# GpSimd computes the low parts of one group's input weights in a two-layer decoder step

## What is computed

```
for i in range(2):                       # layer 0: gated linear attention, layer 1: Mamba-2 SSD
    h = rmsnorm(x, pre_norm[i])
    proj = h @ w_in[i]                   # 1024 -> 3088 (layer 0), 1024 -> 5152 (layer 1)
    # layer 1: split proj into z, xBC, dt; causal conv of width 4 and SiLU on xBC;
    #          chunked scan over tokens with a state per head; y * silu(z); group norm
    y = mixer(proj) @ w_out[i]
    x = x + rmsnorm(y, post_norm[i])
```

## Time and profile before

| | us |
|---|---|
| median of 3 runs | 1502.0 |
| the three runs | 1498.67 to 1502.01 |
| profiled execution, whole | 1505.68 |
| span of its trace | 1503.9 |

### The profile page before, as it was taken

One profiled execution on the slowest core, in us unless ns is written; L12 is line 12 of the kernel. 1 busy time (PEld: TensorE's weight loads), 2 busy tenths in 40 slices (PEclk: granted clock), 3 DMA queues, 4 the chain that ended last, 5 costly groups with the idle time before them and its releaser, 6 DMA issues. The chain is left out here.

```text
span 1503.9 us, 31302 instructions
## 1 busy us (share of the span) xinstructions
PE 1417.1 (94%) x11554; PEld 1180.0 (78%) x11554; DVE 1166.2 (78%) x2591; ACT 839.9 (56%) x1877; POOL 239.0 (16%) x424
## 2 busy tenths in 40 slices
PE   5999999799999979999999999979999999999987
PEld 5889887667888759988888888767777777777765
DVE  4556587758877986898887898995879777588786
ACT  4745555366556545556665764663746556464453
POOL 5010122001422100121110221120112211000002
PEclk8999999999999979999999999999999999999999
DMA  6474567356576434448844764853585674555463
GB/s 191 126 227 136 169 175 219 98 165 189 140 194 204 123 98 131 144 108 229 240 131 134 238 181 124 243 143 86 168 247 156 161 216 119 167 158 174 132 190 64
DMA packets 283874, 245.77 MB, mean 163 GB/s; under 512 B 32664, under 2 KB 250876, under 8 KB 283052
## 3 DMA queue, kind: packets, MB, share of 16 engines
q1 hardware_dynamic: 273628, 209.36, 47.2%
q0 software_dynamic: 10096, 34.41, 8.7%
HBM read 183.02 MB, written 65.00 MB: 165 GB/s over the span
## 5 line engine op out<-in xcount | busy, mean ns | idle before, releaser
L1482 PE MATMUL bank<-h,w 128*128 128x268 f32 (+1 forms) x4752 | 836.0, 330 | 19.2 <-ACT w L867 13.0
L1482 PEld LDWEIGHTS bank<-h,w 128*128 128x128 f32 x4752 | 701.2, 191 | 96.9 <-issue 22.8
L883 DVE TENSOR_TENSOR w<-w_raw,w 128x1024 fp32r<-128x1024 f32 x132 | 160.9, 1219 | 42.9 <-ACT w L867 42.6
L852 PE MATMUL bank<-s_w_out,s_yt_hi 128*128 128x512 f32 (+2 forms) x544 | 168.1, 398 | 2.0 <-DVE s_ys L2600 1.7
L867 ACT ACTIVATE w<-w_raw 128x1024 fp32r<-128x1024 f32 x132 | 138.7, 1051 | 7.8 <-DMA w_raw<-in_ssd_w_in_dram 7.7
L1560 DVE SCALAR_TENSOR_TENSOR conv<-before_conv,cw,conv 128x260 f32<-128x260 f32 (+2 forms) x216 | 125.3, 580 | 4.3
L852 PEld LDWEIGHTS bank<-s_w_out,s_yt_hi 128*128 128x128 f32 (+2 forms) x544 | 95.9, 180 | 28.6 <-issue 2.5
L852 PE MATMUL bank<-g_w_out,g_ot_hi 128*128 128x512 f32 (+2 forms) x288 | 98.0, 429 | 1.7 <-DVE g_ot_lo L2118 1.7
L852 PE MATMUL bank<-s_w_out,s_yt_lo 128*128 128x512 f32 x240 | 94.7, 395 | 0.0
L2363 ACT ACTIVATE s_decay<-s_decay,t_ac 128x128 f32<-128x128 f32 (+1 forms) x288 | 85.5, 379 | 1.2
L1528 ACT ACTIVATE conv<-bank,cw 128x268 f32<-128x268 f32 (+1 forms) x72 | 45.8, 637 | 67.1 <-PE bank L1482 48.7
(11 more groups left out here) (259 smaller groups left out, 2460.7 us busy)
## 6 DMA issues: line engine op xcount, KB each, us to landing
w_raw<-in_ssd_w_in_dram SPq DMA_DIRECT2D x80, 512.0 KB, 4.3
w_raw<-in_gla_w_in_dram SPq DMA_DIRECT2D x48, 512.0 KB, 4.4
s_decay<-kept_acd SPq DMA_DIRECT2D x32, 512.0 KB, 6.3
w_raw<-in_ssd_w_out_dram SPq DMA_DIRECT2D x30, 512.0 KB, 4.2
g_chunk<-kept_gq SPq DMA_DIRECT2D x32, 448.0 KB, 5.4
s_chunk<-kept_sq SPq DMA_DIRECT2D x32, 384.0 KB, 4.8
kept_sq<-stage SPq DMA_DIRECT2D x80, 134.0 KB, 4.5
kept_sq<-stage SPq DMA_DIRECT2D x40, 256.0 KB, 4.9
```

Of the source, the lines that this page charges most:

```text
L852: last = pe.matmul(bank[0:r, :], yt[a][:, k, 0:r], wo[:, b, 512 * half:512 * half + 512], start=(k + a + b == 0), stop=(k == tiles - 1 and ...
L883: dve.tensor_tensor(self.part(i, 1), self.raw(i), hi, ALU.subtract).then_inc(self.w_lo, 1)
L1482: last = pe.matmul(bank[:, 0:n], w[:, p.tile % 2, a, k, :], h[:, b, k, c:c + n], start=(i == 0), stop=(i == len(terms) - 1))
```

## The change

The low parts of layer 1 group 0's 41 input tiles are made by GpSimd, with the same subtraction on the same operands. All other low parts, among them the output weights of that group, stay on VectorE. GpSimd's subtractions count up a semaphore of their own, `pool_lo`. Whoever waits for a low part (TensorE ahead of its 17th matmul, TensorE in the output products, SyncE before a reload) now waits through `wait_low`, which picks the semaphore by the tile and counts the low parts of that kind up to it. The task keeps its place in the list.

```
@@ gpsimd program
             if name == "piece" and at == [10, 0]:
                 gla.prepare(pool)
                 gla.first_samples(pool)
+            elif name == "low" and W.by_pool(*at):
+                W.pool_low(pool, *at)
@@ vector program
-            if name == "low":
+            if name == "low" and not W.by_pool(*at):
                 W.low(dve, *at)
@@ Weights
+    def by_pool(self, i):
+        kind, w = self.plan.weights[i]
+        return kind == "in" and self.plan.tiles[w][0:2] == (1, 0)
+
+    def wait_low(self, engine, i):
+        same = sum(self.by_pool(q) == self.by_pool(i) for q in range(i + 1))
+        engine.wait_ge(self.pool_lo if self.by_pool(i) else self.w_lo, same)
@@ Weights.load
         elif i >= RAW:
-            sp.wait_ge(self.w_lo, i - RAW + 1)
+            self.wait_low(sp, i - RAW)
@@ Weights.out_products
-                pe.wait_ge(self.w_lo, self.index[("out", (L, G, u, k))] + 1)
+                self.wait_low(pe, self.index[("out", (L, G, u, k))])
@@ Weights
+    def pool_low(self, pool, i):
+        pool.wait_ge(self.w_hi, i + 1)
+        pool.tensor_tensor(self.part(i, 1), self.raw(i), self.part(i, 0).bitcast(F32), ALU.subtract).then_inc(
+            self.pool_lo, 1)
@@ Pieces.project
-                pe.wait_ge(self.W.w_lo, self.W.index[("in", p.tile)] + 1)
+                self.W.wait_low(pe, self.W.index[("in", p.tile)])
```

More of the change, by code:

```diff
@@ L779, in __init__ @@
         self.raw_in = [sem(f"raw_in{i}") for i in range(RAW)]
-        self.w_hi, self.w_lo = sem("w_hi"), sem("w_lo")
+        self.w_hi, self.w_lo, self.pool_lo = sem("w_hi"), sem("w_lo"), sem("w_pool_lo")
         self.index = {w: i for i, w in enumerate(plan.weights)}
```

## The result

| | before | after |
|---|---|---|
| median of the runs | 1502.01 us (1498.67 to 1503.57, 4 runs) | 1532.25 us (1530.57 to 1533.24, 4 runs) |
| ratio, 95% interval | 1 | 1.0197 (1.0181 to 1.0214) |
| span of the profiled execution | 1503.9 us | 1531.2 us |
| mean granted clock of TensorE | 0.981 | 0.974 |

The kernel became 30 us slower. The forecast was 1505 us with a range up to 1514 us, so it was wrong by 27 us.

A forecast was written before the change was run, and what follows sets the result against it. TensorE, busy 94% of the span, was taken as the bound. Three places at +1.4, +1.8 and +1.2 us less 0.7 us gave +3.7 us on the 1502.0 us median: 1505.7, rounded down to 1505 us, range 1495 to 1514.

The forecast's parts named there:

- GpSimd's time: Length of each of the 41 subtractions of 128x1024 on GpSimd: 2.3 us, worked out from two smaller GpSimd instructions.
- second rival: GpSimd's instruction is longer, up to 3.7 us, so the kernel takes 1510 to 1514 us; slower cases together 0.34.
- other 38: The moved subtractions outside the three places on TensorE's path: taken as covered by three banks, at no cost.
- 1.08 us of the earlier trace: At 857.27 us a 0.19 us GpSimd operation took 1.08 us beside VectorE's subtraction; taken to show waiting in both directions.
- 54 us read off: VectorE's total wait, from placing 2.3 us subtractions at the 41 high parts in the timeline: 0 to 2.3 us each.
- three places: At 674, 723 to 726 and 771 us TensorE waits for VectorE behind a moved subtraction: +1.4, +1.8 and +1.2 us.
- shrinking gaps: Sign to check: gaps at 674, 726 and 771 us grow by 1 to 2 us; if they shrink, VectorE doesn't wait.
- balance of equal amounts: On VectorE, about 54 us of waits replace the 50.0 us of subtractions removed, so on the whole it gets nothing.
- 0.7 us had been counted as gained: TensorE's waits on the low-part subtraction L883, 0.7 us in all, would vanish; waits on GpSimd under 1 us.
- third rival: GpSimd's order makes low parts late behind samples or roots: +8 us at 41 x 0.2 us; little chance, within slower's 0.34.
- two DMA issues: Behind a sample's state update GpSimd's subtraction stands behind two issues of 0.76 us each; the added wait costed at nothing.
- TensorE's work plus its gaps: Sets the program's length: TensorE busy 94% of the span; the change removes none of its instructions, so only gaps count.

The follow-up runs named there:

- second: The changed kernel, but GpSimd makes the 41 low parts of layer 1's second group and VectorE those of the first; 1508.6 us.
- fourth: The changed kernel, but GpSimd makes the low parts of only every fourth input weight of the first group, 10 of the 41; ratio 1.0035.
- relief: The kernel before, but VectorE computes only 8 of 1024 values of each of the 41 low parts, the rest not computed; 1491.6 us.
- block: The kernel before, all low parts on VectorE, with GpSimd subtracting a 128x512 tile from itself twice beside each of the 41, for nobody; 1539.1 us.
- late: The changed kernel with GpSimd's low parts cut to 8 of 1024 values and four 128x512 fills on GpSimd ahead of each; 1500.3 us.
- queue: The changed kernel, but GpSimd computes only 8 of 1024 values of each of the 41 low parts; 1490.5 us.
- write: The kernel before, with GpSimd filling a 128x512 tile four times beside each of the 41 subtractions, reading nothing from SBUF; 1505.6 us.

## Why the prediction was wrong

**Right: GpSimd's time.** Worked out at 2.3 us each, measured 2.34, 2.40 and 3.47 us (shortest, median, longest):

```profile
L892 POOL TENSOR_TENSOR w<-w_raw,w x41: 2340/2397/3472, 517.7 to 994.8; 128x1024 fp32r<-128x1024 f32 x41
```

So the second rival's condition (from 2.6 us on) wasn't met; the loss came at the duration that had been forecast. That rival's last sentence (at 2.3 us the same side is reached if one more of the other 38 blocks reaches TensorE) names what happened, but it gave it no price of its own; the rival's highest price was 1514 us.

**Right: VectorE waits, by about as much as it is relieved.** The 1.08 us of the earlier trace rows did mean a symmetrical hold. The 54 us read off were 66.4 us. Taps up to 3.44 us appear, where 2.8 had been named. Some 14 us of them are copies from SBUF to SBUF (six in the trace), which the placing by hand had let pass since they have one input. The Trainium skill, page "SBUF — State Buffer", section "Who interferes with whom", says that copies and `tensor_scalar` can enter a mode that uses both ports, and contend with GpSimd in it, while two inputs contend only with a GpSimd instruction that reads SBUF. The runs agree: a copy was held by a fill (0.55 us for 0.16), a two-input tap was not, and a `tensor_scalar` was held by a subtraction (2.51 us for 0.47, in second). The prediction had cited the section for its one half and not for the other.

**Wrong, and the step that failed: "The other 38 I take as covered by the three banks between TensorE and the piece's evacuation."** It put 38 holds at nothing. They cost the larger part: of the 27 us, the three places that were read closely hold 10, and the other 17 lie elsewhere, for instance at 687 to 699 us, where a tap of 3.44 us reached TensorE as a wait of 2.54 us for ScalarE.

Nor are the three places right one by one. They were forecast at +1.4, +1.8 and +1.2 us and took +3.8, +4.2 and +2.1 us. Two of the three gaps that should have grown got smaller, since TensorE had been stopped just ahead of them, and by GpSimd's late low part: the gap at 674 us went from 1.70 to 0.68 us behind a new one of 3.14 us, and the gap at 725.90 us went from 2.14 to 1.68 us behind one of 2.43 us. Only the third grew at its place, from 1.22 to 3.33 us (a copy ahead of the tap was held there as well, from 784.68 us on in the trace of after). The prediction had said that shrinking gaps would mean that VectorE doesn't wait; that sign was badly chosen, as the stretched instructions show.

```profile
735.00 1.98 PE L1499 MATMUL bank<-h,w 128*128 128x268 f32 x8 [2.43 <-POOL w L892]
...
741.57 1.71 PE L1499 MATMUL bank<-h,w 128*128 128x268 f32 x6 [1.68 <-DVE stage L1566]
```

Why the banks didn't cover the 38 is known in part. What is late in the tap chain is late on ScalarE's queue, and so in the next high part: that is shown at 687 to 699 us. That the price hangs on the stretch is shown by second (0.20 against 0.7 per us). That VectorE's being busy 85% of the time is what makes this stretch dear, and not some other difference of the two groups, is argued, not shown. That holds add up because the next one comes some 11 us later isn't needed: in fourth they lie 33 us and more apart and still cost 0.6 us for each stretched one.

**Wrong: the balance of equal amounts.** "On the whole VectorE gets nothing" was read as near zero for TensorE. relief and block show that the two sides don't weigh the same: 41 us of work taken away gave back 9.8 us, 0.2 for each, and 51 us of holds took 37, 0.7 for each. A likely reason, not tested: the subtraction lay in VectorE's order where the plan had put it, with slack around it, while the hold falls on whatever is next when the high part is done.

**Wrong: lateness "at nothing".** The waits on the low part didn't vanish (0.7 us had been counted as gained), they are 5.9 us, in four places, where under 1 us had been forecast. In the largest, 3.14 us, the subtraction stood behind a norm root that waited for ScalarE, as the third rival had it; in the next, 2.43 us, behind a sample's two DMA issues, which the prediction had put at nothing. What they are worth in the kernel's time is open. late and queue leave about 4 us, with an uncertainty as large, and late has only 2.3 us of such waits. The rival that named it had given its price (+8 us) by order alone, which queue puts at nothing.

**Wrong: TensorE's own work taken as fixed.** The prediction started from "the program is as long as TensorE's work plus its gaps" and costed only the gaps. For the same 11554 matmuls TensorE was busy 1430.6 us against 1417.1 us. So of the 27.3 us between the two traces half, 13.5 us, lies in matmuls that lasted longer, and half in gaps. The cause is the granted clock. From 664 to 673 us of the kernel after it is 1.00; behind the gap of 3.14 us, from 673 to 679 us, it is 0.72, that is, for part of the window TensorE ran at 1.2 in place of 2.4 GHz. Three more such stretches follow, beside or behind gaps of 2.54, 2.43 and 3.33 us:

```profile
664.00:673.00 9.00, 6.43 (x50) 6.08 (x48) 8.79 (x19) 3.83 (x10) 3.51 (x3) 1.00 0.12 37
673.00:679.00 6.00, 5.43 (x31) 5.43 (x32) 4.42 (x13) 4.33 (x12) 1.02 (x4) 0.72 0.49 133
...
701.00:708.00 7.00, 7.00 (x38) 6.81 (x36) 5.91 (x16) 2.73 (x9) 1.07 (x2) 0.51 0.71 172
735.00:745.00 10.00, 6.50 (x27) 5.82 (x28) 8.44 (x16) 6.89 (x17) 1.86 (x1) 0.51 0.35 102
790.00:797.00 7.00, 5.73 (x26) 5.65 (x27) 6.30 (x16) 2.43 (x6) 0.00 (x0) 0.52 0.52 125
```

Worked out from these shares, some 27 us there ran at 1.2 GHz; in before it is 7 us for the same part of the program (0.76 over 700 to 707 us and 0.66 over 725 to 730 us).

Executions of one kernel differ in the clock too, so the two traces alone don't give the change's share. All the executions on record do. The kernel before has 0.980 to 0.991 in the 78 executions of the four groups, 0.985 in the mean; after has 0.974 to 0.983 in four (mean 0.979), block 0.973 to 0.977 in four, all below the lowest of the 78. As (1 - clock) x span that is 23 us missing before, 33 us in after and 38 us in block, which differs from before by GpSimd's extra work only. So the holds bring the lower clock with them, and about 10 us of clock, an estimate from these means, belongs to the change. The 0.7 us for each held microsecond has this in it.

## What to carry to other kernels

Before work is moved from VectorE to GpSimd, look at what both read: a GpSimd instruction that reads SBUF stops VectorE's two-input instructions and SBUF-to-SBUF copies for its whole length, so 50 us of relief became 66 us of waiting. Don't set relief against hold one to one, and don't sum the path over the places where TensorE already waits: a microsecond of hold cost 0.7 us in a stretch where VectorE was busy 85% of the time and 0.2 us in another, it can surface on a third engine several instructions later, and about a third of the loss (an estimate) came as a lower TensorE clock. Such a move can be priced ahead by a run that does the new engine's work for nobody (block) and one that leaves the old engine's out (relief); here their sum, +27 us, came near the result of +30 us.

## What the runs showed of the hardware that was not expected

- The wait of one engine for the other is written into the length of the waiting instruction, on both engines, and not as idle time: a tap of 0.50 us reads 3.44, GpSimd's subtraction of 2.34 reads 3.47. A group whose mean grows while its work hasn't changed is the sign.
- A VectorE instruction can be caught before GpSimd's subtraction has begun by the trace, when a DMA issue of GpSimd runs just ahead of it: the tap at 731.86 us lasted 3.39 us, the subtraction only from 732.59 to 734.95. The issue alone doesn't do it: in before, the tap at 718.54 us keeps 0.50 us beside the issue at 718.50 us, with no long subtraction behind it. So a hold can last longer than the subtraction by about an issue.

```profile
731.82 0.76 POOL L2328 DMA_DIRECT2D s_sample_state<-in_state_ssm_dram  x1
732.59 2.36 POOL L892 TENSOR_TENSOR w<-w_raw,w 128x1024 fp32r<-128x1024 f32 x1
...
731.86 3.39 DVE L1577 SCALAR_TENSOR_TENSOR conv<-before_conv,cw,conv 128x268 f32<-128x268 f32 x1
```

- SBUF-to-SBUF copies of VectorE of 128x3 and 32x32 are held by GpSimd's fills (20 copies in write, 7.2 us), instructions with two SBUF inputs are not (one, 0.2 us).
- Cutting GpSimd's instruction in four made the holds shorter but more in number: 52.3 us stretched over 85 instructions in place of 66.4 us over 35, and the time is the same within the intervals (1.0182 and 1.0197).
